# Moving the per-pair preparation of an RWKV-7 recurrence out of the pairs' loop and beside the weight projections

## The reference, cut to what matters

```python
def odd_layer(x, mu, w_r, w_k, w_v, w_g, w0, w1, w2, a0, a1, a2, k_k, k_a, r_k, gn_w, gn_b, w_o):
    ...
    r, k, v, g = xr @ w_r, xk @ w_k, xv @ w_v, xg @ w_g
    w_log = -softplus(-(w0 + tanh(xw @ w1) @ w2)) - 0.5
    decay = exp(-exp(w_log))                       # = exp(-e^-0.5 * sigmoid(...))
    a = sigmoid(a0 + (xa @ a1) @ a2)
    kk = (k * k_k).reshape(B_, S, H, N)
    kk = kk / maximum(sqrt(sum(kk * kk, axis=-1)), L2_EPS)
    k = k * (1.0 + (a - 1.0) * k_a)
    o = wkv7_scan(r, decay, k, v, kk, a)           # state of 64 x 64 per head, 512 steps
    o = group_norm(o) * gn_w + gn_b
    bonus = sum(r * k * r_k, axis=-1) * v
    o = (o + bonus) * silu(g)
    return o @ w_o
```

## Time and profile before

| | us |
|---|---|
| median of 3 runs | 3456.24 |
| lowest and highest run | 3447.67, 3457.91 |
| the profiled execution's own time | 3451.87 |
| its span, first to last instruction | 3450.2 |
| the 16 projection groups | about 2100 to 2816 on the trace |
| the pairs' loop | about 2817 to 3238 |

### The profile page before, as it was taken

One profiled execution on the slowest core, in us unless ns is written; L12 is line 12 of the kernel. 1 busy time (PEld: TensorE's weight loads), 2 busy tenths in 40 slices (PEclk: granted clock), 3 DMA queues, 4 the chain that ended last, 5 costly groups with the idle time before them and its releaser, 6 DMA issues.

```text
span 3450.2 us, 51623 instructions
## 1 busy us (share of the span) xinstructions
PE 3324.1 (96%) x20934; PEld 2666.6 (77%) x20934; DVE 1828.3 (53%) x2381; ACT 1419.9 (41%) x1623; POOL 411.2 (12%) x724
## 2 busy tenths in 40 slices
PE   7999999999999999999999999999999989999897
PEld 1678888888887888888888867888888867777685
DVE  7666666666667233444423456242424247787545
ACT  2343544443444233444422235141414157777423
POOL 0001222232212000000000000000000024443000
PEclk8999999999999999999999999999999999999998
DMA  9423232233322432222222313333333433333322
GB/s 372 172 78 102 88 106 94 88 111 109 106 99 93 165 132 88 80 79 86 87 88 100 119 62 138 122 122 122 122 122 122 135 88 89 73 87 65 128 98 73
DMA packets 178668, 380.41 MB, mean 110 GB/s; under 512 B 111696, under 2 KB 117072, under 8 KB 144720
## 3 DMA queue, kind: packets, MB, share of 16 engines
q1 hardware_dynamic: 164064, 325.69, 28.3%
q0 software_dynamic: 14448, 52.50, 4.5%
HBM read 341.44 MB, written 35.13 MB: 109 GB/s over the span
## 4 chain that ended last, share of the span: by engine, by line
PE 86%; DVE 5%; DMA 3%; ACT 2%; SPq 2%; POOLq 1%; issue 1%; DVEq 1%; ACTq 0%; POOL 0%
PE PJ L319 18%; PE PJ L321 18%; PE PJ L320 18%; PE AB L320 6%; PE AB L319 6%; PE AB L321 6%; PE AB L1770 1%; PE AB L1761 1%; DMA WK<-ada 1%; POOLq L1663 1%; POOLq L1666 1%; DMA WS<-solved_scratch 1%; PE AB L493 1%; PE AB L545 1%; PE AB L1300 0%
## 5 line engine op out<-in xcount | busy, mean ns | idle before, releaser
L319 PE MATMUL PJ<-XH,WH 128*128 128x512 f32 x2816 | 1112.0, 395 | 13.6 <-DVE XL L467 6.2
L321 PE MATMUL PJ<-XH,WL 128*128 128x512 f32 x2816 | 1098.6, 390 | 0.0
L320 PE MATMUL PJ<-XL,WH 128*128 128x512 f32 x2816 | 1098.4, 390 | 0.0
L352 DVE TENSOR_TENSOR WL<-RAW,WH 128x2048 fp32r<-128x2048 f32 (+1 forms) x234 | 538.6, 2302 | 676.2 <-ACT WH L348 672.2
L348 ACT ACTIVATE WH<-RAW 128x2048 fp32r<-128x2048 f32 (+1 forms) x236 | 449.3, 1904 | 859.6 <-PE PJ L321 605.3
L319 PEld LDWEIGHTS PJ<-XH,WH 128*128 128x128 f32 x2816 | 530.0, 188 | 123.8 <-issue 15.9
L321 PEld LDWEIGHTS PJ<-XH,WL 128*128 128x128 f32 x2816 | 529.7, 188 | 111.7
L320 PEld LDWEIGHTS PJ<-XL,WH 128*128 128x128 f32 x2816 | 530.3, 188 | 108.6 <-issue 2.2
L319 PE MATMUL AB<-XH,WH 128*128 128x512 f32 (+1 forms) x960 | 380.8, 397 | 9.6 <-DVE XL L467 7.7
L321 PE MATMUL AB<-XH,WL 128*128 128x512 f32 (+1 forms) x960 | 375.4, 391 | 0.0
L320 PE MATMUL AB<-XL,WH 128*128 128x512 f32 (+1 forms) x960 | 375.2, 391 | 0.0
(11 more groups left out here) (477 smaller groups left out, 3937.5 us busy)
## 6 DMA issues: line engine op xcount, KB each, us to landing
RAW<-w SPq DMA_DIRECT2D x232, 1024.0 KB, 4.9
WK<-ada SPq DMA_DIRECT2D x32, 1024.0 KB, 7.3
GATE<-gate POOLq DMA_DIRECT2D x64, 256.0 KB, 3.0
rkvg_scratch<-WK POOLq DMA_DIRECT2D x16, 1024.0 KB, 4.9
x_scratch<-X POOLq DMA_DIRECT2D x8, 1024.0 KB, 5.7
X<-rkvg_scratch SPq DMA_DIRECT2D x32, 256.0 KB, 3.6
RAW<-rkvg_scratch SPq DMA_DIRECT2D x32, 256.0 KB, 3.3
X<-xT SPq DMA_DIRECT2D x4, 1024.0 KB, 15.7
```

The costliest lines, as they stand in the source:

```text
L319: nc.tensor.matmul(bank[0:width, n, :], hi, xh, start=first, stop=False)
L320: nc.tensor.matmul(bank[0:width, n, :], hi, xl, start=False, stop=False)
L321: m = nc.tensor.matmul(bank[0:width, n, :], lo, xh, start=False, stop=last)
L352: nc.vector.tensor_tensor(WL[k % 2][:, :, 0:w], narrow(RAW[k % 2], w), WH[k % 2][:, :, 0:w].bitcast(F32), ALU.subtract).then_inc(wl_ready, 1)
```

## The change

The preparation leaves the pairs' loop.

- Groups 0 to 2 and 4 to 6 (`RATE_PAIRS`, two or three pairs each): PE makes the low-rank products of those pairs (`rate_pe`) in the PSUM banks that the previous group has left, now in split precision (three matmuls of rounded operands for each of the two products, as in the projections); ACT does the sigmoids, POOL stores decay rate and a to the DRAM scratch `rates_scratch`.
- Groups 8 to 10 and 12 to 14 (`KEY_PAIRS`): SP loads k, r and a of the pairs back; ACT, DVE and PE make the key norms, scaled keys and bonus sums (`key_act`, `key_dve`, `key_squares_pe`, `key_bonus_pe`, two matmuls of rounded operands for each sum); POOL stores four tiles for each pair to `factors_scratch`.
- Groups 12 to 15 (g): ACT copies the result out through Silu, both halves (`gate_act`); DVE has no part in it.
- The pairs' loop loads, for each pair, seven tiles of 256 KB (`sp_load`) and, three iterations later, the gate (`sp_load_gate`), where it loaded four tiles and the low-rank piece. All preparation steps are gone from `wv_pe`, `wv_act`, `wv_dve`, `first_pe`, `first_act` and `first_dve`, and some waits of the steps that stay are on other semaphores.
- The hardware loops over the groups are written out, instruction by instruction.

```diff
+        RATE_PAIRS = {0: range(0, 3), 1: range(3, 6), 2: range(6, 8), 4: range(8, 11), 5: range(11, 14), 6: range(14, 16)}
+        KEY_PAIRS = {8: range(0, 3), 9: range(3, 6), 10: range(6, 9), 12: range(9, 12), 13: range(12, 14),
+                     14: range(14, 16)}
...
+        def rate_pe(pe, n, k):
...
+            for i in (range(2) if k == 0 else range(2, np_) if k == 2 else ()):
...
+                for j in range(2):
+                    at, to = slice(j * w + i * P, j * w + (i + 1) * P), spare(n)[:, 2 * (i % 2) + j, :]
+                    th, tl = (a[:, j * SEQ:(j + 1) * SEQ] for a in (TWA_HI, TWA_LO))
+                    nc.tensor.matmul(to, LW_HI(2 * w)[:, at], th, start=True, stop=False)
+                    nc.tensor.matmul(to, LW_HI(2 * w)[:, at], tl, start=False, stop=False)
+                    m = nc.tensor.matmul(to, LW_LO(2 * w)[:, at], th, start=False, stop=True)
...
+        def key_bonus_pe(pe, n):
+            for i in range(len(KEY_PAIRS[n])):
+                pe.wait_ge(s("prep_dve"), key_dve_done(n, IN_BLO, i))
+                nc.tensor.matmul(spare(n)[:, i, :], ONES64, unit(i, U_HI, True), start=True, stop=False)
+                m = nc.tensor.matmul(spare(n)[:, i, :], ONES64, unit(i, U_KEY, True), start=False, stop=True)
+            m.then_inc(s("prep_products"), 1)
...
         def sp_load(sp, q):
+            if q >= 2:
+                sp.wait_ge(wv(f"in{q % 2}"), gate_loaded(q - 4) if q >= 4 else pair_loaded(q - 2))
+                sp.wait_ge(wv("bv"), q - 1)
+                sp.wait_ge(wv("tok"), token_done(q - 2, 2))
+            for dst, a in ((LOGW(q), rates_d[q, 0]), (AKK(q), facts_d[1, q]), (ws(T_IN(q) + T_R), rkvg_d[0, q]),
+                           (ws(T_IN(q) + T_KK), facts_d[0, q]), (ws(T_IN(q) + T_K2), facts_d[2, q]),
+                           (ws(T_IN(q) + T_V), rkvg_d[2, q]), (BONUS(q), facts_d[3, q])):
+                sp.dma_start(dst, a).then_inc(wv(f"in{q % 2}"), 16)
...
-            for m in range(4):
-                sp.dma_start(ws(T_IN(q) + m), rkvg_d[m, q]).then_inc(wv(f"in{q % 2}"), 16)
...
-            at(t + 3, lambda q: sp_load_lora(sp, q), 3)
             at(t + 1, lambda q: sp_solved_back(sp, q), 1)
             at(t + 2, lambda q: sp_blocks_in(sp, q), 2)
             at(t + 2, lambda q: sp_levels(sp, q), 2)
+            at(t + 1, lambda q: sp_load_gate(sp, q), 1)
             at(t + 4, lambda q: sp_load(sp, q), 4)
```

More of the change, by code:

```diff
@@ L1745, in pe_r1 @@
             i.then_inc(wv("r1"), 1)
-        def pe_bonus(pe, q):
-            pe.wait_ge(wv("factors"), 4 * q + 3)
-            wait(pe, wv("o"), q - 1)
-            nc.tensor.matmul(bank(0), mat("ones64"), ws(T_BONUS), start=True, stop=True).then_inc(wv("bonus"), 1)
         def pe_level_w(pe, v, l):
@@ L2285, in _ @@
             w_load_lora(G_LORA)
-            with sp.Fori(G_RW, G_OUT3 - 1) as G:
-                w_load(G, G_QI + 1)
+            for n in range(15):
+                w_load(G_RW + n, G_QI + 1)
+                if n in RATE_PAIRS:
+                    rate_load(sp, n)
+                elif n in KEY_PAIRS:
+                    keys_load(sp, n)
             def w_load_g(k):
@@ L2893, in _ @@
                       next_split=lambda dve, G, k: None)
-            with dve.Fori(0, 3) as m:
-                for g in range(4):
-                    dve_group(dve, G_RW + 4 * m + g, rw_dve(dve, 4 * m + g, (PJ, AB)[g % 2]),
-                              steps=(lambda k: k < SLOTS and mix_dve(dve, 6 + m, k)) if g == 3 else None)
             nc.vector.tensor_scalar(OMKA, COL[:, COLS["k_a"]:COLS["k_a"] + KT], -1.0, 1.0, ALU.mult, ALU.add)
```

404 lines of the change are left out of this document (244 added, 160 removed).

## The result

The changed kernel takes 3578.43 us (median of four runs, 3576.88 to 3585.84), the kernel before 3457.07 (four runs, 3447.67 to 3460.34). The ratio is 1.0367, with a 95% interval of 1.0348 to 1.0385: 121 us slower, where +58 was forecast, and outside the range that ended at 3532. The profiled execution took 3576.88, with a span of 3575.2 us against 3450.2, so there are 125.0 us between the two traces to account for.

A forecast was written before the change was run, and what follows sets the result against it. TensorE was taken to bound the projections, a cycle of SP and POOL the pairs' loop. The terms 36.2 + 4 - 6.0 + 1 + 24 - 1 = +58.2 us on the profiled 3451.9 gave 3510 us, range 3468 to 3532.

The forecast's parts named there:

- The removed TensorE work in the loop buys nothing: Pairs' loop: no matmul is in the cycle of SP and POOL, so 3.4 us less TensorE work an iteration wins nothing.
- Matmuls added to the projections, +36.2: Projection groups: 160 added matmuls at 0.226 us each, with no TensorE gap to hide under, cost +36.2 us.
- I take +4 us over the six key groups: Key groups of the projections: TensorE's waits for preparation cost +4 us in all, with ends of 0 and 12.
- three places in a key group: Key groups: TensorE would wait for the squares, the bonus products and the bank if other engines' work were not hidden.
- my tightest place: Bonus products in a key group: a chain of about 19 us where TensorE takes about 20 to come to it.
- Group 15, -6.0 + 1: Last projection group: seven full-precision products removed win 6.0 us; the last gate copy, all on ScalarE, costs 1 us.
- The second cycle, 25.8 to 28.4, taken at 27.5: Pairs' loop: levels, loads and solve write set the period, 25.8 if the clock holds, 28.4 if it falls; +24 us.
- POOL's solve, -0.7: Pairs' loop: less VectorE contention shortens POOL's solve by 0.7 us, with ends of 0 and -2.8.
- up to 2.8: POOL's solve: VectorE's work costs it up to 2.8 us, from 15.4 us in the loop against 12.6 for pair 0.
- That the clock holds (3490): Rival for the pairs' loop: loads lengthen the cycle to 25.8 us but the clock holds; 3490 us, chance 0.15.
- that the solve cycle alone sets the pace (3470): Rival for the pairs' loop: extra loads hide while SP waits for POOL, period 24.3 us; 3470 us, chance 0.23.
- the faster one: Rival for the pairs' loop: it was bound by TensorE after all and wins 48 us; 3439 us, chance 0.09.

The follow-up runs named there:

- The mended kernel: Changed kernel with loop loads issued later, low-rank loads ahead of slot-3 weights, rate products later and pairs regrouped in the projections: 3498.60 us, ratio 1.0123.
- the later loads: Changed kernel with seven loads of a pair issued behind the read of the blocks, not between level writes and solve write: 3543.85 us, ratio 1.0256.
- the early low-rank loads: Changed kernel with the low-rank load of each rate group issued ahead of that group's slot-3 weight load: 3566.33 us, ratio 1.0316.
- the small loads: Changed kernel with the loop's loads from pair 4 on, except the gate load, cut to 64 of 512 columns: 3562.56 us, ratio 1.0310.

## Why the prediction was wrong, step by step

**The removed TensorE work in the loop buys nothing.** Right, and shown from two sides: less of it in the kernel before costs 0.4% (7 of 16 us in the loop itself), more of it in the changed kernel gains 12 us.

**Matmuls added to the projections, +36.2.** Right. Groups that don't wait are longer by 0.227 us for each of their matmuls (47.70 for 18).

**"I take +4 us over the six key groups."** This is the step that failed. I had written that "without that cover TensorE waits at three places in a key group", and costed only those; the loads I had put down as "hidden by VectorE's and ScalarE's idle two thirds", which is no cover for a load. What an idle engine hides is compute. A load is hidden if it is issued early enough, and where it stands in SP's queue is in the code: behind slot 3 of the weights, due after slot 0. The rate groups were taken to cost nothing beyond matmuls. The term measured 84.7 - 36.2 = 48.5 us in place of 4: 38.6 us of waits, 27.1 of them for the low-rank operands (5 of these, in group 0, still with the making of the activations), and about 10 for the matmuls that follow a wait at the lower clock. The bonus products, my tightest place, don't appear among the waits; the squares do (7.4 us, in groups 8 and 12), again for a load: in group 8 ScalarE waited 9.52 us for the tiles of the group's pairs. The mended kernel gives back 38.7 us of it by moving loads and products alone.

**Group 15, -6.0 + 1.** Measured -4.6.

**The second cycle, 25.8 to 28.4, taken at 27.5.** Mechanism right, size short: 28.73, above the upper end too. From the first load to the landed write it took 10.6 us on the mean of the twelve (forecast 10.1). The rest of the cycle was forecast at 15.7 plus two thirds of 2.6, 17.4 in all, and measured 28.7 - 10.6 = 18.1, where 15.7 + 2.6 is 18.3. So of the 1.2 us that were missing in the period 0.5 are the loads and 0.7 the clock, which takes its full price on the mean: a wait three times as long had been seen in no row, and I took a mean between ends. The 12 iterations cost 38.6 us for the 24 of the forecast.

**POOL's solve, -0.7.** From its first instruction to its last it went from 14.9 us on the mean of the twelve iterations to 13.2, so -1.7, within its ends. In the changed kernel this is lost, since POOL waits for SP. The Trainium skill, "GPSIMD Engine Reference", Key points, says that GpSimd contends with VectorE instructions that read two SBUF inputs; the trace agrees in direction, 13.2 against 14.9 with less of them about. The 12.6 us were no undisturbed solve, though: for pair 0 the same instructions take 11.2 us in the changed kernel, with VectorE busy for 0.4 us of them where it was for 2.3, so "up to 2.8" was too small a figure for what VectorE's work can cost POOL.

**The rivals.** That the clock holds (3490), that the solve cycle alone sets the pace (3470), and the faster one all fell: SP waited for POOL in 2 iterations of the changed kernel's 15. The ends of the range were made of ends of single terms; no term had a place for loads that come late in the rate groups, so 3532 could not hold the time. (The sum behind that end was off as well: 3510 + 8 + 11 is 3529, so the two ends would not pass 3532 even together.)

## What to carry to other kernels

Work that is moved beside a bound engine brings its loads with it, and each load needs its own check: where it stands in the issuing queue, what is in front of it, and when its first reader is due. When a loop is a cycle of small transfers through memory, bulk loads belong in the queue behind the cycle's last transfer, where the next engine works on its own, and not directly in front of a small write that the cycle waits for (25.22 us an iteration here against 28.73), provided that their buffers are free at that place (where they were not, it was 29.33). Before removing work from TensorE, look at what its waits will do to the clock: here five of the six waits from 3.0 to 10.8 us in the projections were followed by matmuls at half speed.

## What the runs showed of the hardware

A small write behind large loads on one queue waits for their bytes: 3.5 us from issue to landing as seen by POOL, 6.2 behind 2 MB, 3.7 with seven of the eight loads cut to an eighth and as many issues. The Trainium skill, "DMA: Bandwidth & Descriptors", section on queues, rings and completion order, says that on each DMA engine the descriptors of a ring are consumed in ring order; these numbers agree with it, but no run put the write on another queue, so the order on the queue and the sharing of the DMA engines are not told apart.

Added matmuls made a kernel faster (12 us for 48 us of added work), and removed ones made it slower (0.4%). The Trainium skill, "TensorE: Matmul & The Clock Gate", section on HAM oscillation, describes a clock that falls between bursts in each round of a loop; the changed kernel's 0.83 agrees. What a fall costs has to be read on the path: with the later loads the way to the levels took up to 11.0 us, and the solve write still went as POOL ended.

Unexpected was the end of the loop. The rest of the program behind `sp_solved_out` of pair 15 takes 247.8 us before and 247.4 to 248.5 in three others, the changed kernel among them, but 254 to 257 in the remaining eight, with the same waits of TensorE where I compared them. The first 20 us behind it, for the changed kernel and the one with the loads later:

```profile
3327.00:3347.00 20.00, 14.14 (x385) 12.14 (x386) 9.47 (x18) 7.23 (x10) 0.00 (x0) 1.00 0.46 150
```

```profile
3287.00:3307.00 20.00, 16.18 (x329) 13.75 (x328) 8.81 (x17) 6.42 (x10) 0.00 (x0) 0.68 0.45 150
```

The same part of the program runs at a granted clock of 1.00 in one and 0.68 in the other. In all twelve traces the two go together: 1.00 over these 20 us in the four with the short tail, 0.63 to 0.79 in the eight with the long one. It is most of why the later loads gained 42 us in the loop and 35 in the kernel. What decides between the two courses is open; it is not the clock of the loop's last 20 us alone, which was 0.83 in the changed kernel (short tail), 0.83 with the early low-rank loads (long) and 1.00 with the small loads (long). Each kernel has one trace, so it is also open whether the course goes with the kernel or with the single execution.
